# Two transfers per staged unit, and one reload per query tile, in a two-layer transformer kernel

## The chip, the cores and the metric

The kernel runs on one core of a Trainium2 chip. The core has TensorE (PE, matmuls), VectorE (DVE), ScalarE (ACT), GpSimd (POOL) and SyncE (SP), which only issues transfers, and 16 DMA engines that move data between HBM and the on-chip memory SBUF. Matmuls write to PSUM, eight banks of 128 x 512 floats. Transfers are issued from two queues here: SyncE's (q1 in the profile) and ScalarE's (q10). An engine works through its queue in order, so an instruction that waits, or a transfer being issued, holds what is behind it. The metric is the device time of one execution in microseconds.

## The reference

One sequence of 2048 tokens by 1024 features in float32 goes through two blocks. The part that the change touches is the first block's attention:

```
p = rmsnorm(x, norm1_g) @ w_in                 # 1024 -> u 256, dq dk dv 512 each, sq sk sv 256 each
a = pool_mixer(u)                              # trailing means, a small map per group
b = diff_attention(dq, dk, dv)                 # 4 heads: softmax(q1 k1^T) - lam * softmax(q2 k2^T), times v
c = stick_breaking_attention(sq, sk, sv)       # 4 heads of 64
x = x + concat(a, b, c) @ w_out
x = x + (silu(h2 @ w_gate) * (h2 @ w_up)) @ w_down      # h2 = rmsnorm(x, norm2_g)
x = rmsnorm(x, final_norm_g)
```

Both attentions are causal and scale by 1/8. The second block is a gated MLP over 128-token chunks and a retention branch, with a projection in and one out.

## The kernel before, in words

The sequence is cut in 4 chunks of 512 tokens. Matmuls keep float32 accuracy by splitting each operand in a rounded part (hi, written by ScalarE) and the rest (lo, VectorE's or GpSimd's subtraction) and adding three products: lines L1503, L1504 and L1505. Weights come as halves: `load_w` (L2620, L2627, SyncE) brings a raw half of 512 KB into one of three slots of RAW, `split_w` rounds it on ScalarE (L1749) and subtracts on GpSimd (L2529) into one of four or five places. `load_w` of half n waits for the split of half n-3. From about 1426 us on, halves that were kept in HBM are fetched again ready made (`fetch_w`, L2641, 1024 KB).

The projections of all four chunks come first (until about 580 us). A unit is one PSUM bank of 128 x 512 results. For a query or key unit (`store_qk`), ScalarE writes hi (L1823) and VectorE lo (L2135) into one of four slots of STG, hi in the first 512 columns of a slot, lo in the next; the 128 partitions hold two heads of 64 features each. Value units of the second attention are written the same way (`store_v`, L1831 and L2143); value units of the first attention stay whole. Then ScalarE's queue stores the slot to HBM scratch: `put_qk` (L1844 for queries, L1847 for keys) and `put_v` (L1861). One put is held back until the next unit is done (`put_later`).

- Queries: 4 transfers per unit, one for each of hi, lo and each head, into QS[6, 16, 64, hi/lo, head, 128].
- Keys: 4 transfers, into KS[6, 4, 128, head, 512], hi on the first 64 rows, lo on the last 64.
- Split values: 8 transfers, for hi/lo, head pair and 128-token tile.

There are 24 query units, 24 key units and 8 split value units. The attention goes over 96 tiles (4 chunks x 6 head pairs x 4 blocks of 128 queries). For each tile `load_q` (L2681, SyncE) brings the same 64 rows of 512 floats twice, onto partitions 0 to 63 and 64 to 127 of one of three slots of QQ, with two transfers. `load_k` (L2665) brings keys with hi on partitions 0 to 63 and lo on the others, and `scores` multiplies: QQ's hi part and then its lo part as the stationary side against hi and lo keys together (L1613, L1614). The softmax exponentials are on ScalarE (L1869), the turned probabilities are split by ScalarE (L1882) and VectorE (L2226).

The order of the work is one list, made when the program is built. The projections and everything after them run as one generator, `projections`, the attention as a second, `attention`. At each of 1484 places of the first, HALF_STEPS says how many half steps of the second are put there. Each engine takes its own instructions from this list in this order, and SyncE its transfers.

Of the kernel before, what the change touches and what calls it, by code (L numbers as in the profile page):

```python
# [9 lines left out]
F32 = mybir.dt.float32  # L10
# [3 lines left out]
ACT = mybir.ActivationFunctionType  # L14
ALU = mybir.AluOpType
# [4 lines left out]
CT = 512  # L20
NC = S // CT
# [50 lines left out]
class Signals:  # L72
# [6 lines left out]
    def inc(self, name, event, by=1):  # L79
        if name not in self.sems:  # L80
            self.sems[name] = self.ctx.enter_context(self.nc.semaphore(name))
        self.count[name] = self.count.get(name, 0) + by
        self.at[event] = (name, self.count[name])
        return self.sems[name], by

    def landed(self, name, event):
        return self.inc(name, event, 16)
# [127 lines left out]
def attention_cost(c):  # L215
# [2 lines left out]


HALF_STEPS = (  # L220
    "0000000000000000000000000000000000000000000000001200110120000010020200100101000000000100100100101210"
    "2122110001011003015000021100000020021110111002101121110100100021010011010111016100002001012010102002"
    "0001001000000001010000000000110222100210001001010000001110000220211002000100001010003002002010110101"
    "0010130131701131020000001011001000101001000001010000022021200210100010100000012000000201000010110001"
    "0031121021100110100001000001000100200001011020002130422112020001102020200000000000000000001000001010"
    "0001021000101010001010010011002010100000000010200000000111002001100100100100101111100000001100110000"
    "1002000200000000102001000010000000010102001003120111001221110011202022000011504100001010100000011000"
    "1011102000101001000000000011002000100011001120010000112020100101001000100001000102001002000212011102"
    "0021212001000100101010001011011000200100110012201210111200000100101000200110100300100002010022011010"
    "0010022100010010000100001000001001000011000010210100012000000001000002200000000000001111100000010000"  # L230
    "0000010000000101001000100020011001210002200201011000200000001200200000002001100200101200002100010200"
    "0101200021002000010020200211000100002111110002002200200110000000200210000001100010000101011211302400"
    "1000000001010011101000011000110100100311201031210000000001010001000100101000100000001001011101002000"
    "0010100000110101000010001002212100321110020000000000000000000000000010000000000100102010001201200111"
    "001100200120012100100010012001000001010120001010011102000101101110000000320100221004"
)


# [1070 lines left out]
def build(nc, I, const, out, scr):  # L1309
    with ExitStack() as ctx:  # L1310
        def sbt(name, n, dt=F32, stack=ctx):
            return stack.enter_context(nc.sbuf_tensor(name, [128, n], dt))

        BIG = sbt("BIG", 8192, FR)
        with ExitStack() as lay:
            STG = sbt("STG", 4096, FR, lay)
# [23 lines left out]
        PS = [ctx.enter_context(nc.psum_tensor(f"PS{i}", [128, 512], F32)) for i in range(8)]  # L1340
# [51 lines left out]
        QS, KS, VS, VW, US, YS, GP, GWS, WS, TB = [scr[n] for n in ("QS", "KS", "VS", "VW", "US", "YS", "GP", "GWS", "WS", "TB")]  # L1392
# [45 lines left out]
        def stage(s):  # L1438
            return STG[:, 1024 * s:1024 * s + 512], STG[:, 1024 * s + 512:1024 * s + 1024]

        def keys_of(kb):
            return KV[:, 2048 * kb:2048 * kb + 1024]

# [3 lines left out]
        def queries(s):  # L1447
            return QQ[:, 512 * s:512 * s + 512]
# [47 lines left out]
        inc, landed = sig.inc, sig.landed  # L1496


        def tensor_program(pe):
# [105 lines left out]
            def scores(c, x, r, j, qt, kb, w, ks, q, b, before):  # L1605
                for e in before:
                    on.wait_ge(*e)
                on.wait_ge("k", c, j, kb)
                on.wait_ge("q", c, j, qt)
                kk = keys_of(ks).rearrange("p (r t) -> p r t", r=2)  # L1610
                qq = queries(q).rearrange("p (a r t) -> p a r t", a=2, r=2)
                o = PS[4 + b][:, 0:w]
                pe.matmul(o, qq[:, 0, r, :], kk[:, r, 0:w], start=True, stop=False)  # L1613
                pe.matmul(o, qq[:, 1, r, :], kk[:, r, 0:w], start=False, stop=True).then_inc(*inc("scored", ("sc", x, r)))  # L1614
# [119 lines left out]
        def scalar_program(act):  # L1734
# [84 lines left out]
            def store_qk(c, u, kind, b, s, sbefore, ft):  # L1819
                on.wait_ge("mm", u)  # L1820
                for e in sbefore:
                    on.wait_ge(*e)
                act.activation(stage(s)[0], PS[b][:, :], ACT.Identity,  # L1823
                               scale=0.125 if kind == "q" else 1.0).then_inc(*inc("qkv_hi", ("qh", u)))

            def store_v(c, u, b, s, sbefore, ft, g):
                on.wait_ge("mm", u)
                for e in sbefore:
                    on.wait_ge(*e)
                to = stage(s)[0] if ft == 4 else stage(s)[0].bitcast(F32)  # L1830
                act.activation(to, PS[b][:, :], ACT.Copy).then_inc(*inc("qkv_hi", ("qh", u)))  # L1831

            def put_u(c, u, s, f):
                on.wait_ge("uc", u)
# [2 lines left out]
            def put_qk(c, u, kind, s, ft):  # L1837
                on.wait_ge("qh", u)
                on.wait_ge("ql", u)
                for a, src in enumerate(stage(s)):  # L1840
                    for r in range(2):
                        rows = src[64 * r:64 * r + 64, :].bitcast(F32)
                        if kind == "q":
                            act.dma_start(QS[ft, 4 * c:4 * c + 4, :, a, r, :].rearrange("q d t -> d q t"),  # L1844
                                          rows.rearrange("d (q t) -> d q t", q=4)).then_inc(*landed(f"s_st{s}", ("qst", u)))
                        else:
                            act.dma_start(KS[ft, c, 64 * a:64 * a + 64, r, :], rows).then_inc(*landed(f"s_st{s}", ("qst", u)))  # L1847

            def put_v(c, u, s, ft, g):
                on.wait_ge("qh", u)  # L1850
                if ft < 4:
                    act.dma_start(VW[:, c, :, g, :].rearrange("h p e -> p h e"),
                                  stage(s)[0].bitcast(F32).rearrange("p (h e) -> p h e", h=4)).then_inc(*landed(f"s_st{s}", ("qst", u)))
                    return
                on.wait_ge("ql", u)
                for a, src in enumerate(stage(s)):
                    for f in range(2):
                        view = src.rearrange("p (u n) -> p u n", u=2)[:, :, 128 * f:128 * f + 128]
                        by_head = VS[f, c, :, :, :, :].rearrange("p t a e -> p (t a e)").rearrange("p (t r a e) -> p t r a e", t=4, r=2, a=2)
                        for i in range(2):  # L1860
                            act.dma_start(by_head[:, 2 * g + i, :, a, :],  # L1861
                                          view[:, i, :].rearrange("p (r e) -> p r e", r=2).bitcast(F32)).then_inc(*landed(f"s_st{s}", ("qst", u)))

            def soft_exp(x, r, m, kb, w, b, s, before, m_after):
                nm, sm, _ = norm_cols(m, 4 * r + kb, 1)
# [141 lines left out]
        def vector_program(dve):  # L2007
# [122 lines left out]
                dve.tensor_copy(stage(s)[0].bitcast(F32), PS[b][:, :]).then_inc(*inc("u_out", ("uc", u)))  # L2130

            def store_qk(c, u, kind, b, s, sbefore, ft):
                hi, lo = stage(s)
                on.wait_ge("qh", u)
                dve.scalar_tensor_tensor(lo, PS[b][:, :], 0.125 if kind == "q" else 1.0, hi.bitcast(F32), ALU.mult,  # L2135
                                         ALU.subtract).then_inc(*inc("qkv_lo", ("ql", u)))

            def store_v(c, u, b, s, sbefore, ft, g):
                if ft < 4:
                    return  # L2140
                hi, lo = stage(s)
                on.wait_ge("qh", u)
                dve.tensor_tensor(lo, PS[b][:, :], hi.bitcast(F32), ALU.subtract).then_inc(*inc("qkv_lo", ("ql", u)))  # L2143

            def pool_load(c, u_stored, free):
                for e in free:
# [423 lines left out]
        def sync_program(sp):  # L2570
# [106 lines left out]
            def load_q(c, j, qt, s, after):  # L2677
                for e in after:
                    on.wait_ge(*e)
                for d in range(2):  # L2680
                    sp.dma_start(queries(s)[64 * d:64 * d + 64, :].bitcast(F32),  # L2681
                                 QS[j, 4 * c + qt, :, :, :, :].rearrange("d a r t -> d (a r t)")).then_inc(
                                     *landed(f"s_q{s}", ("q", c, j, qt)))

            def store_head(c, j):
                on.wait_ge("fm", c, j)
# [152 lines left out]
```

## Time and profile before

| | |
|---|---|
| median of 3 runs | 3711.91 us (3709.17 to 3713.26) |
| the profiled execution | 3712.05 us |
| its span, first to last instruction | 3710.3 us |
| mean granted TensorE clock | 0.988 |
| busy: PE, PEld, DVE, ACT, POOL | 97%, 83%, 51%, 45%, 22% of the span |
| SyncE's DMA queue q1 | 725.02 MB, 56.4% of 16 engines |
| ScalarE's DMA queue q10 | 35.67 MB, 3.5% of 16 engines |

PE is TensorE's matmuls, PEld its weight loads. Transfers being issued do not count as busy time of ScalarE or SyncE, though they keep its queue. A DMA share of 1 would be all 16 DMA engines with a packet in work all the time.

### The profile page before, as it was taken

What the parts mean: (1) busy time and instruction counts of PE and PEld (TensorE: products, weight loads), DVE (VectorE), ACT (ScalarE), POOL (GpSimd) and SP (SyncE); (2) the same over time, 40 slices, a digit from 0 to 9 for tenths busy, and PEclk for the clock granted to TensorE, in tenths of its full rate; (3) what the DMA queues carried; (4) which work ended last, traced back from release to release, by engine and by line L of the source; (5) the groups of instructions that cost most, each with busy time, mean ns of one, the idle gap of its engine ahead of it and who ended that gap; (6) DMA issues with size and microseconds to landing.
All of it is one profiled execution on the core that took longest, in us unless ns stands there. A gap on an engine that the chain in (4) does not pass through costs nothing.

```text
span 3710.3 us, 50941 instructions
## 1 busy us (share of the span) xinstructions
PE 3589.8 (97%) x19284; PEld 3081.8 (83%) x19284; DVE 1907.8 (51%) x4043; ACT 1664.5 (45%) x3393; POOL 807.5 (22%) x704
## 2 busy tenths in 40 slices
PE   7899999999999999999999999999999999999999
PEld 6788888777887898888888998888888988888788
DVE  4255654566657765445646555435477752111443
ACT  4344545545666454545544344435456532111322
POOL 3344443444454432000011011110000000000100
PEclk9999999999999999999999999999999999999999
DMA  6787677787776667545455456454454464555454
GB/s 191 215 251 214 187 216 275 258 283 268 267 255 227 239 230 288 188 165 196 167 183 177 165 204 216 160 203 170 165 213 136 150 240 184 190 183 205 171 189 153
DMA packets 328454, 763.95 MB, mean 206 GB/s; under 512 B 53265, under 2 KB 204817, under 8 KB 271890
## 3 DMA queue, kind: packets, MB, share of 16 engines
q1 hardware_dynamic: 267410, 725.02, 56.4%
q10 hardware_dynamic: 60800, 35.67, 3.5%
q8 instruction: 154, 2.52, 0.3%
q14 instruction: 90, 0.74, 0.1%
HBM read 586.25 MB, written 174.35 MB: 205 GB/s over the span
## 4 chain that ended last, share of the span: by engine, by line
PE 77%; DVE 5%; DMA 2%; ACT 2%; issue 1%; POOL 1%; SPq 0%; ACTq 0%; DVEq 0%
PE PS L1503 21%; PE PS L1505 21%; PE PS L1504 21%; PE PS L1622 3%; PE PS L1632 2%; PE PS L1613 2%; PE PS L1614 2%; PE PS L1646 2%; DMA XS<-in_w_ada 1%; PE PS L1581 1%; POOL WF L2529 1%; DVE XS L2309 0%; DVE BIG L2109 0%; ACTq L1861 0%; PE PS L1705 0%
## 5 line engine op out<-in xcount | busy, mean ns | idle before, releaser
L1503 PE MATMUL PS<-BIG,WF 128*128 128x512 f32 (+1 forms) x1792 | 688.4, 384 | 13.5 <-ACT BIG L1815 6.1
L1505 PE MATMUL PS<-BIG,WF 128*128 128x512 f32 (+1 forms) x1792 | 677.0, 378 | 0.0
L1504 PE MATMUL PS<-BIG,WF 128*128 128x512 f32 (+1 forms) x1792 | 676.6, 378 | 0.0
L2529 POOL TENSOR_TENSOR WF<-RAW,WF 128x512 fp32r<-128x512 f32 x380 | 509.3, 1365 | 620.0 <-ACT WF L1749 620.0
L1503 PE MATMUL PS<-WF,BIG 128*128 128x512 f32 (+1 forms) x1760 | 626.0, 356 | 8.2 <-DVE BIG L2098 4.6
L1505 PE MATMUL PS<-WF,BIG 128*128 128x512 f32 (+1 forms) x1760 | 611.3, 347 | 0.0
L1504 PE MATMUL PS<-WF,BIG 128*128 128x512 f32 (+1 forms) x1760 | 610.3, 347 | 0.0
L1503 PEld LDWEIGHTS PS<-BIG,WF 128*128 128x128 f32 x1792 | 343.0, 191 | 73.7 <-ACT BIG L1815 7.4
L1505 PEld LDWEIGHTS PS<-BIG,WF 128*128 128x128 f32 x1792 | 342.2, 191 | 62.9
L1504 PEld LDWEIGHTS PS<-BIG,WF 128*128 128x128 f32 x1792 | 343.2, 191 | 58.1
L1503 PEld LDWEIGHTS PS<-WF,BIG 128*128 128x128 f32 x1760 | 336.4, 191 | 52.3 <-ACT BIG L1799 5.2
L1505 PEld LDWEIGHTS PS<-WF,BIG 128*128 128x128 f32 x1760 | 336.1, 191 | 42.7
L1504 PEld LDWEIGHTS PS<-WF,BIG 128*128 128x128 f32 x1760 | 337.0, 191 | 40.4 <-issue 1.9
L1869 ACT ACTIVATE PP<-PS,SM 128x512 f32<-128x512 f32 (+3 forms) x320 | 199.1, 623 | 360.4 <-DVE SM L2194 349.7
L2556 POOL TENSOR_TENSOR AT<-XS,AT 128x512 fp32r<-128x512 f32 x88 | 115.9, 1317 | 1113.4 <-ACT AT L1932 1113.4
L1749 ACT ACTIVATE WF<-RAW 128x1024 fp32r<-128x1024 f32 x190 | 198.5, 1053 | 129.7 <-issue 90.4
L2194 DVE TENSOR_REDUCE SM<-PS 128x1 f32<-128x512 f32 (+3 forms) x320 | 193.2, 607 | 117.0 <-PE PS L1614 112.5
L2283 DVE TENSOR_TENSOR XH<-PS,XH 128x512 f32<-128x512 f32 x224 | 150.3, 686 | 199.9 <-PE PS L1505 199.8
L1932 ACT ACTIVATE AT<-XS 128x512 fp32r<-128x512 f32 x88 | 55.6, 632 | 397.9 <-DVE XS L2288 397.9
L1503 PE MATMUL PS<-WF,AT 128*128 128x512 f32 x584 | 233.5, 400 | 0.3 <-POOL WF L2529 0.3
L1505 PE MATMUL PS<-WF,AT 128*128 128x512 f32 x584 | 228.5, 391 | 0.0
L1504 PE MATMUL PS<-WF,AT 128*128 128x512 f32 x584 | 227.8, 390 | 0.0
(233 smaller groups left out, 6259.6 us busy)
## 6 DMA issues: line engine op xcount, KB each, us to landing
WF<-scratch_WS SPq DMA_DIRECT2D x264, 1024.0 KB, 5.0
scratch_WS<-WF SPq DMA_DIRECT2D x110, 1024.0 KB, 6.7
W<-scratch_WS SPq DMA_DIRECT2D x66, 1024.0 KB, 5.0
RAW<-in_w_in SPq DMA_DIRECT2D x84, 512.0 KB, 4.6
KV<-scratch_KS SPq DMA_DIRECT2D x60, 512.0 KB, 5.9
QQ<-scratch_QS SPq DMA_DIRECT2D x192, 128.0 KB, 5.1
XH<-in_x SPq DMA_DIRECT2D x32, 512.0 KB, 7.4
scratch_QS<-STG ACTq DMA_DIRECT2D x96, 128.0 KB, 4.0
```

Source lines behind the costliest of these rows:

```text
L1503: pe.matmul(o, Ah, Bh, start=first, stop=False)
L1504: pe.matmul(o, Ah, Bl, start=False, stop=False)
L1505: return pe.matmul(o, Al, Bh, start=False, stop=last)
L1613: pe.matmul(o, qq[:, 0, r, :], kk[:, r, 0:w], start=True, stop=False)
L1614: pe.matmul(o, qq[:, 1, r, :], kk[:, r, 0:w], start=False, stop=True).then_inc(*inc("scored", ("sc", x, r)))
L1622: m = pe.transpose(PS[6][:, 128 * i:128 * i + 128], src[:, 128 * i:128 * i + 128], ident)
L1749: act.activation(half_of(n)[0], rawp(n), ACT.Copy).then_inc(*inc("w_hi", ("w_hi", n)))
L1869: act.activation(probs(s)[:, 0:w], PS[4 + b][:, 0:w], ACT.Exp, bias=nm, accum_out=sm).then_inc(*inc("p_exp", ("ex", x, r)))
L2194: dve.tensor_reduce(nm, PS[4 + b][:, 0:w], AX, ALU.max, negate=True).then_inc(*inc("row_max", ("mx", x, r)))
L2283: dve.tensor_tensor(dst, PS[b][:, :], dst, ALU.add).then_inc(*inc("residual", ("res", u)))
L2529: pool.tensor_tensor(lo, rawp(n)[:, 512 * i:512 * i + 512], hi.bitcast(F32), ALU.subtract).then_inc(*inc("w_lo", ("w_lo", n, i)))
L2556: pool.tensor_tensor(lo, gated(s), hi.bitcast(F32), ALU.subtract).then_inc(*inc("act_lo", ("al", u)))
```

## The change

1. Queries: ScalarE and VectorE write the staged unit as four query blocks of 128 with hi and lo side by side in each, so that one transfer per head stores both: 2 per unit. The scratch becomes QS[6, 16, 64, head, 256], and `scores` reads QQ as (head, hi/lo, token) in place of (hi/lo, head, token).
2. Keys: staged as before; one transfer per head stores hi and lo: 2 per unit. The lo part is a plain subtraction now.
3. Split values: staged as eight blocks of 64 with hi and lo side by side; one transfer per head pair: 2 per unit.
4. `load_q` is one transfer. Its source is the 64 rows with a leading dimension of 2 and a step of 0, its destination all 128 partitions.
5. HALF_STEPS has other digits at 366 of its 1484 places; their sum is 742 in both.

```diff
+        def stage_parts(s):
+            return STG[:, 1024 * s:1024 * s + 1024]
+
+        def stage_q(s):
+            q4 = stage_parts(s).rearrange("p (q a t) -> p q a t", q=4, a=2)
+            return q4[:, :, 0, :], q4[:, :, 1, :]
+
+        def stage_v(s):
+            m8 = stage_parts(s).rearrange("p (m a e) -> p m a e", m=8, a=2)
+            return m8[:, :, 0, :], m8[:, :, 1, :]
...
-                qq = queries(q).rearrange("p (a r t) -> p a r t", a=2, r=2)
+                qq = queries(q).rearrange("p (r a t) -> p a r t", a=2, r=2)
...
-                for a, src in enumerate(stage(s)):
-                    for r in range(2):
-                        rows = src[64 * r:64 * r + 64, :].bitcast(F32)
-                        if kind == "q":
-                            act.dma_start(QS[ft, 4 * c:4 * c + 4, :, a, r, :].rearrange("q d t -> d q t"),
-                                          rows.rearrange("d (q t) -> d q t", q=4)).then_inc(*landed(f"s_st{s}", ("qst", u)))
-                        else:
-                            act.dma_start(KS[ft, c, 64 * a:64 * a + 64, r, :], rows).then_inc(*landed(f"s_st{s}", ("qst", u)))
+                for r in range(2):
+                    rows = stage_parts(s)[64 * r:64 * r + 64, :].bitcast(F32)
+                    if kind == "q":
+                        act.dma_start(QS[ft, 4 * c:4 * c + 4, :, r, :].rearrange("q d x -> d q x"),
+                                      rows.rearrange("d (q x) -> d q x", q=4)).then_inc(*landed(f"s_st{s}", ("qst", u)))
+                    else:
+                        act.dma_start(KS[ft, c, :, r, :].rearrange("(a d) t -> d a t", a=2),
+                                      rows.rearrange("d (a t) -> d a t", a=2)).then_inc(*landed(f"s_st{s}", ("qst", u)))
...
-                for a, src in enumerate(stage(s)):
-                    for f in range(2):
-                        view = src.rearrange("p (u n) -> p u n", u=2)[:, :, 128 * f:128 * f + 128]
-                        by_head = VS[f, c, :, :, :, :].rearrange("p t a e -> p (t a e)").rearrange("p (t r a e) -> p t r a e", t=4, r=2, a=2)
-                        for i in range(2):
-                            act.dma_start(by_head[:, 2 * g + i, :, a, :],
-                                          view[:, i, :].rearrange("p (r e) -> p r e", r=2).bitcast(F32)).then_inc(*landed(f"s_st{s}", ("qst", u)))
+                view = stage_parts(s).rearrange("p (i f x) -> p i f x", i=2, f=2).bitcast(F32)
+                for f in range(2):
+                    act.dma_start(VS[f, c, :, 2 * g:2 * g + 2, :, :].rearrange("p i a e -> p i (a e)"),
+                                  view[:, :, f, :]).then_inc(*landed(f"s_st{s}", ("qst", u)))
...
-                dve.scalar_tensor_tensor(lo, PS[b][:, :], 0.125 if kind == "q" else 1.0, hi.bitcast(F32), ALU.mult,
-                                         ALU.subtract).then_inc(*inc("qkv_lo", ("ql", u)))
+                if kind == "q":
+                    hi, lo = stage_q(s)
+                    dve.scalar_tensor_tensor(lo, PS[b][:, :].rearrange("p (q t) -> p q t", q=4), 0.125, hi.bitcast(F32), ALU.mult,
+                                             ALU.subtract).then_inc(*inc("qkv_lo", ("ql", u)))
+                else:
+                    hi, lo = stage(s)
+                    dve.tensor_tensor(lo, PS[b][:, :], hi.bitcast(F32), ALU.subtract).then_inc(*inc("qkv_lo", ("ql", u)))
...
-                for d in range(2):
-                    sp.dma_start(queries(s)[64 * d:64 * d + 64, :].bitcast(F32),
-                                 QS[j, 4 * c + qt, :, :, :, :].rearrange("d a r t -> d (a r t)")).then_inc(
-                                     *landed(f"s_q{s}", ("q", c, j, qt)))
+                src = QS[j, 4 * c + qt, :, :, :].rearrange("(b d) r x -> b d (r x)", b=1).broadcast_to([2, 64, 512])
+                sp.dma_start(queries(s).bitcast(F32), src).then_inc(*landed(f"s_q{s}", ("q", c, j, qt)))
```

## Rows read from the trace of the kernel before

**Rows 1.** Windows, by stage: window, its us, busy (count) by engine, clock, DMA share, GB/s.
```profile
150.00:465.00 315.00, 289.21 (x1585) 253.46 (x1586) 179.10 (x409) 147.22 (x347) 131.06 (x108) 0.96 0.72 216
465.00:1010.00 545.00, 514.23 (x2604) 433.01 (x2603) 316.67 (x615) 285.61 (x595) 244.23 (x198) 0.97 0.76 260
1010.00:1400.00 390.00, 377.61 (x2217) 329.89 (x2217) 257.20 (x569) 222.61 (x452) 172.24 (x149) 1.00 0.68 235
1400.00:2830.00 1430.00, 1419.52 (x7581) 1215.54 (x7580) 768.45 (x1552) 683.75 (x1443) 155.26 (x164) 1.00 0.54 189
...
sum 3710.00, PE 3589.82 PEld 3081.83 DVE 1907.77 ACT 1664.48 POOL 807.52; mean PE 598.30 PEld 513.64 DVE 317.96 ACT 277.41 POOL 134.59
```
**Rows 2.** Waits of TensorE, 60 to 600 us: in total, times, longest.
```profile
PE PS L1613 <- ACT PP L1869: 7.4, 2, 3.8
...
PE PS L1646 <- DVE PT L2226: 6.2, 2, 4.8
PE PS L1503 <- ACT BIG L1815: 6.1, 1, 6.1
PE PS L1613 <- DMA QQ<-scratch_QS: 4.9, 1, 4.9
```
**Rows 3.** Windows, the four chunk ends of the projections: the first and the sum.
```profile
140.00:180.00 40.00, 28.26 (x190) 27.00 (x190) 18.01 (x32) 11.00 (x22) 11.02 (x8) 0.83 0.73 221
...
sum 160.00, PE 132.85 PEld 123.79 DVE 90.48 ACT 68.84 POOL 58.72; mean PE 33.21 PEld 30.95 DVE 22.62 ACT 17.21 POOL 14.68
```
**Rows 4.** Timeline of ScalarE at two chunk ends: start, us, what, [idle before].
```profile
148.49 15.96 ACTq L1861 DMA_DIRECT2D scratch_VS<-STG  x16
164.50 1.06 ACT L1749 ACTIVATE WF<-RAW 128x1024 fp32r<-128x1024 f32 x1 [15.47 <-issue]
...
436.16 5.26 ACTq L1861 DMA_DIRECT2D scratch_VS<-STG  x8
441.52 0.60 ACT L1882 ACTIVATE PT<-PS 128x512 fp32r<-128x512 f32 x1 [5.11 <-issue]
```
**Rows 5.** Issues of the four transfers: ns min/median/max, first and last start.
```profile
L1844 ACTq DMA_DIRECT2D scratch_QS<-STG x96: 582/640/1230, 41.9 to 550.0; - x96
L1847 ACTq DMA_DIRECT2D scratch_KS<-STG x96: 452/620/1629, 74.8 to 562.0; - x96
L1861 ACTq DMA_DIRECT2D scratch_VS<-STG x64: 364/492/2397, 148.5 to 578.8; - x64
...
L2681 SPq DMA_DIRECT2D QQ<-scratch_QS x192: 444/597/2223, 150.3 to 2804.4; - x192
```
**Rows 6.** The staging writes, same columns.
```profile
L1823 ACT ACTIVATE STG<-PS x48: 577/597/601, 36.9 to 554.0; 128x512 fp32r<-128x512 f32 x48
L2135 DVE SCALAR_TENSOR_TENSOR STG<-PS,STG x48: 674/691/693, 37.5 to 554.6; 128x512 fp32r<-128x512 f32 x48
```
**Rows 7.** Issue to landing of query loads (L2681), then of weight fetches (L2641).
```profile
DMA to landing us min/median/max: 2.4/5.1/13.9
...
DMA to landing us min/median/max: 4.6/5.0/13.6
```
**Rows 8.** DMA in 1794 to 1799 us: packets, MB, share of 16 engines.
```profile
q1 hardware_dynamic: 160, 0.26, 19.3%
```
**Rows 9.** DMA, 150 to 465 us, two rows, then 465 to 1010 us, one.
```profile
q1 hardware_dynamic: 36125, 48.31, 49.3%
...
QQ<-scratch_QS SPq DMA_DIRECT2D x49, 128.0 KB, 5.1
...
QQ<-scratch_QS SPq DMA_DIRECT2D x48, 128.0 KB, 6.5
```
**Rows 10.** Weight splits and raw loads: the splits, SyncE's wait, landing of L2627.
```profile
L1749 ACT ACTIVATE WF<-RAW x190: 1040/1056/1069, 10.9 to 1422.0; 128x1024 fp32r<-128x1024 f32 x190
...
SPq L2627 <- POOL WF L2529: 673.7, 139, 20.8
...
DMA to landing us min/median/max: 2.1/4.4/12.2
```

More of the change, by code:

```diff
@@ L220 @@
 HALF_STEPS = (
[L221 to L225, printed above, removed]
@@ L226 @@
-    "0001021000101010001010010011002010100000000010200000000111002001100100100100101111100000001100110000"
-    "1002000200000000102001000010000000010102001003120111001221110011202022000011504100001010100000011000"
+    "0000000000000000000000000000000000000000000000001011110010001020020000200010100000001020000102100110"
+    "2121100010001202114020301101020000100120111011001121010002000101110101101101111000300210010200100102"
+    "0002000000010200110001010000010122101110001100000000201101100211221001000010000001000002040012100100"
@@ L228 @@
+    "1000231200201740220011000100000000010100100010111001031021210101010002000010010001000010100010001002"
+    "1210020210000200101100000100010100000110001002002021320222200002022012010000100010000000000001000011"
+    "0000102010010010111000000000021001202000000010200001000011000200100000020010001000320000110000110000"
+    "1100200100000010101000001000010000010102001003111111001221110011202022000011504100001010100000011000"
     "1011102000101001000000000011002000100011001120010000112020100101001000100001000102001002000212011102"
-    "0021212001000100101010001011011000200100110012201210111200000100101000200110100300100002010022011010"
@@ L230 @@
-    "0010022100010010000100001000001001000011000010210100012000000001000002200000000000001111100000010000"
-    "0000010000000101001000100020011001210002200201011000200000001200200000002001100200101200002100010200"
+    "0021212001000100101010001011011000200100110012201210101010101100011101011050000100001000211121012011"
+    "0010000100000100000100010001110000000011010001020010002100000001100000200000000000001111101000000000"
+    "0000010000000101001000100020011001100202220101100000200000001200200000002001100200101200002100010200"
@@ L232 @@
     "0101200021002000010020200211000100002111110002002200200110000000200210000001100010000101011211302400"
     "1000000001010011101000011000110100100311201031210000000001010001000100101000100000001001011101002000"
-    "0010100000110101000010001002212100321110020000000000000000000000000010000000000100102010001201200111"
-    "001100200120012100100010012001000001010120001010011102000101101110000000320100221004"
+    "0010100000110010100100200002012202301110000100100000000000000000000100000000000200101102010010200111"
@@ L236 @@
+    "001100200120012100100010012001000000001010101010100200300001011220001001110001112015"
 )
@@ L1822, in store_qk @@
                     on.wait_ge(*e)
-                act.activation(stage(s)[0], PS[b][:, :], ACT.Identity,
-                               scale=0.125 if kind == "q" else 1.0).then_inc(*inc("qkv_hi", ("qh", u)))
+                if kind == "q":
+                    act.activation(stage_q(s)[0], PS[b][:, :].rearrange("p (q t) -> p q t", q=4), ACT.Identity,
+                                   scale=0.125).then_inc(*inc("qkv_hi", ("qh", u)))
+                else:
+                    act.activation(stage(s)[0], PS[b][:, :], ACT.Identity).then_inc(*inc("qkv_hi", ("qh", u)))
             def store_v(c, u, b, s, sbefore, ft, g):
@@ L1829, in store_v @@
                     on.wait_ge(*e)
-                to = stage(s)[0] if ft == 4 else stage(s)[0].bitcast(F32)
-                act.activation(to, PS[b][:, :], ACT.Copy).then_inc(*inc("qkv_hi", ("qh", u)))
+                if ft == 4:
+                    act.activation(stage_v(s)[0], PS[b][:, :].rearrange("p (m e) -> p m e", m=8), ACT.Copy).then_inc(
+                        *inc("qkv_hi", ("qh", u)))
+                else:
+                    act.activation(stage(s)[0].bitcast(F32), PS[b][:, :], ACT.Copy).then_inc(*inc("qkv_hi", ("qh", u)))
             def put_u(c, u, s, f):
@@ L1839, in put_qk @@
                 on.wait_ge("ql", u)
-                for a, src in enumerate(stage(s)):
-                    for r in range(2):
-                        rows = src[64 * r:64 * r + 64, :].bitcast(F32)
-                        if kind == "q":
-                            act.dma_start(QS[ft, 4 * c:4 * c + 4, :, a, r, :].rearrange("q d t -> d q t"),
-                                          rows.rearrange("d (q t) -> d q t", q=4)).then_inc(*landed(f"s_st{s}", ("qst", u)))
-                        else:
-                            act.dma_start(KS[ft, c, 64 * a:64 * a + 64, r, :], rows).then_inc(*landed(f"s_st{s}", ("qst", u)))
+                for r in range(2):
[3 more added lines that the diff above has]
+                                      rows.rearrange("d (q x) -> d q x", q=4)).then_inc(*landed(f"s_st{s}", ("qst", u)))
+                    else:
+                        act.dma_start(KS[ft, c, :, r, :].rearrange("(a d) t -> d a t", a=2),
+                                      rows.rearrange("d (a t) -> d a t", a=2)).then_inc(*landed(f"s_st{s}", ("qst", u)))
             def put_v(c, u, s, ft, g):
@@ L2132, in store_qk @@
             def store_qk(c, u, kind, b, s, sbefore, ft):
-                hi, lo = stage(s)
                 on.wait_ge("qh", u)
-                dve.scalar_tensor_tensor(lo, PS[b][:, :], 0.125 if kind == "q" else 1.0, hi.bitcast(F32), ALU.mult,
-                                         ALU.subtract).then_inc(*inc("qkv_lo", ("ql", u)))
+                if kind == "q":
+                    hi, lo = stage_q(s)
+                    dve.scalar_tensor_tensor(lo, PS[b][:, :].rearrange("p (q t) -> p q t", q=4), 0.125, hi.bitcast(F32), ALU.mult,
+                                             ALU.subtract).then_inc(*inc("qkv_lo", ("ql", u)))
+                else:
+                    hi, lo = stage(s)
+                    dve.tensor_tensor(lo, PS[b][:, :], hi.bitcast(F32), ALU.subtract).then_inc(*inc("qkv_lo", ("ql", u)))
             def store_v(c, u, b, s, sbefore, ft, g):
@@ L2140, in store_v @@
                     return
-                hi, lo = stage(s)
+                hi, lo = stage_v(s)
                 on.wait_ge("qh", u)
-                dve.tensor_tensor(lo, PS[b][:, :], hi.bitcast(F32), ALU.subtract).then_inc(*inc("qkv_lo", ("ql", u)))
+                dve.tensor_tensor(lo, PS[b][:, :].rearrange("p (m e) -> p m e", m=8), hi.bitcast(F32),
+                                  ALU.subtract).then_inc(*inc("qkv_lo", ("ql", u)))
             def pool_load(c, u_stored, free):
@@ L2832 @@
     scr = {}
-    for name, shape in (("QS", [6, 16, 64, 2, 2, 128]), ("KS", [6, NC, 128, 2, CT]), ("VS", [2, NC, 128, 4, 2, 128]), ("VW", [4, NC, 128, 4, 128]),
+    for name, shape in (("QS", [6, 16, 64, 2, 256]), ("KS", [6, NC, 128, 2, CT]), ("VS", [2, NC, 128, 4, 2, 128]), ("VW", [4, NC, 128, 4, 128]),
                         ("US", [2, 128, S + 16]), ("YS", [S, D]), ("GP", [1, D]), ("GWS", [128, 4, 128]), ("WS", [SPLIT - KEPT, 128, 2048]), ("TB", [2, 128, 1024])):
```

## The prediction

> **What bounds the kernel now.** I read the stages first [rows 1], the five of them by busy time, granted clock and DMA share, to see where TensorE leaves time at all. It is busy for 3589.82 of 3710 us, so about 120 us are idle, and they are not spread evenly: from 1400 to 2830 us only 10 us of 1430 are idle, while 150 to 465 us has 25.8 idle of 315 and 465 to 1010 us has 30.8 of 545. Those two stages also have the highest DMA share (0.72 and 0.76, against 0.54 later). The change touches what runs there: the projections store queries, keys and values until about 579 us [rows 5], and the query loads run from 150 to 2804 us.
>
> Next, what TensorE waits for in 60 to 600 us [rows 2]. Four rows matter: 7.4 us for ScalarE's exponentials, 6.2 us for a VectorE piece that itself waited for ScalarE, 6.1 us for ScalarE's rounding of the next activations, and 4.9 us for the first query load. The four 40 us windows at the ends of the projection chunks hold 27.2 us of TensorE idle (160 minus 132.85), 11.7 of them at the first end, where the granted clock is 0.83 [rows 3]. The ScalarE timeline says why [rows 4]: at 148.49 us its queue issues 16 value stores in a row and this takes 15.96 us, with the weight split behind it starting after 15.47 us of idle; at 436.16 us eight of them take 5.26 us and hold the next turned-probability eviction for 5.11 us. So ScalarE's queue, filled by store issues, is what ends waits at the chunk ends. Elsewhere the tensor engine bounds.
>
> **The stores, part by part.** Removed: per query unit 4 issues become 2 (96 to 48), per key unit the same (96 to 48), per split-value unit 8 become 2 (64 to 16). By the medians 48 x 0.640 + 48 x 0.620 + 48 x 0.492 = 84 us of ScalarE queue time before 580 us [rows 5]. For queries and keys no long TensorE wait stands behind the issues, and I give them 0 (0 to 5 us gain). For values, three of four issues go at each chunk end. The waits of TensorE that trace to a late ScalarE there are 7.4 + 6.2 + 6.1 = 19.7 us [rows 2]; three quarters is 15 us gained. Bounds: 5 us, if the pieces queued behind are late for the next reason (VectorE's own lo parts and softmax maxima are next), and 20 us. What is stored has the same bytes. Rows of a value store grow from 256 to 512 bytes and those of a query store from 512 to 1024, which only shortens the queue-10 traffic; 0 to 3 us of DMA engine time, not counted.
>
> The staging writes now go to 4 or 8 blocks in place of one run (query and value units), and the key's subtraction drops a multiply by 1. The nearest rows are the writes themselves, 0.597 us on ScalarE and 0.691 us on VectorE [rows 6]. No row shows the blocked form; at 10% each way over 56 units it is 3 us on either engine, hidden under TensorE's gemms at all but the chunk ends. I take 0, plus or minus 1.
>
> **The query reload.** Two issues of 128 KB become one of 256 KB, 192 to 96, 0.6 us of SyncE each [rows 5]; SyncE mostly waits for a free buffer, so this is worth 0 (at best half a microsecond on the first load). But the shape of the source changes. Before, each transfer counts 64 rows outermost. In a quiet stretch [rows 8] two such loads left 160 packets: 128 rows of 2 KB, and 32 more, 16 for each load, so each one ran on all sixteen DMA engines. The new source counts 2 outermost, with a step of 0, then 64 rows; only below it lie the equal parts that sixteen engines would need. No row of before shows such a transfer. The two ends are: still sixteen engines, then nothing is lost; or one half per engine, then two engines carry 128 KB each where each engine carried 16 KB per tile before. I take the second, because in the rows each of these loads is split by its outermost count.
>
> What that second end costs. Two engines get 112 KB more per tile. Price from three rows. Slope between landings: a 1024 KB fetch has 64 KB per engine and lands at best in 4.6 us, a 128 KB query load has 8 KB and lands at best in 2.4 us [rows 7], so 56 KB take 2.2 us and 112 KB take 4.4 us. The SyncE queue's own rate in this stage: 48.31 MB in 49.3% of 16 x 315 us is 19.4 GB/s per engine, so 5.9 us [rows 9]. The quiet stretch: 0.26 MB in 19.3% of 16 x 5 us is 17 GB/s, 6.8 us [rows 8].
>
> Stage 150 to 465 us: an engine is in use for 0.72 x 315 = 227 us [rows 1]. 49 issues are 24.5 tiles [rows 9]. The two engines then need 227 + 24.5 x 4.4 = 335 us up to 227 + 24.5 x 5.9 = 372 us, which is 20 to 57 us more than there are; I take the middle, 38. Every transfer of the queue, weights and keys too, lands only when those two engines have done their share, so their backlog delays all. What TensorE has in hand against it is the lead of the weight loads: there are three raw slots, so a load goes out when the split three before it is done (SyncE waits 673.7 us for that), 190 splits in 1411 us is 7.4 us each, two of them are 15 us, less 4.4 us of landing: 10 us of lead [rows 10]. So 38 - 10 = 28 us lost. Bounds: 0 if the other packets get quicker once fourteen engines are idler, and 79 us at 6.8 us without any lead.
>
> First tile: TensorE already waits 4.9 us for it [rows 2]; it lands about 5 us later, +5 (0 to 7).
>
> Stage 465 to 1010 us: 0.76 x 545 = 414 us, plus 24 tiles at 4.4 to 5.9 is 520 to 556 us of 545 [rows 1, 9]. Full but not clearly over, with the lead already spent: +8 (0 to 32). Stage 1010 to 1400: about 13 tiles, 0.68 x 390 + 13 x 5.9 = 342 of 390, fits. After that 0.54 and the queries of one tile are needed far later than loaded: 0.
>
> ScalarE waits in order for a raw weight, so when one is late its exponentials are late too; that multiplies stalls and is why I don't go to the low end.
>
> The Trainium skill speaks against the new reload, in "DMA: Bandwidth & Descriptors", the table of rules for kernel authors and the section on why a DMA increments its semaphore by 16: the engines used are the largest number up to 16 that divides the slowest dimension of both sides, and a leading zero-stride broadcast of c copies keeps the whole transfer on at most c engines. That is 2 here. The count of 16 small packets per load agrees with it for 64 rows; that a count of 2 gives two engines no row of before can show.
>
> **The places.** 366 of 1484 digits of the order string differ, the sum is 742 in both, and at no slot is the attention more than 8 half steps behind or 5 ahead of its old position. It moves pieces against each other at the scale of single waits. All of TensorE's idle time is 120 us, and a part of it is what such a move can shift; I take 0, between -6 and +8.
>
> **Sum.** 28 + 5 + 8 - 15 = +26 us. The profiled execution took 3712.05 us (span 3710.3, 1.75 around it), which is 0.1 above the median 3711.91. So 3738 us.
>
> **Rivals.** Below 0.2% (7.4 us) no difference from no change can be told.
> (A) Forecast, the two engines back up: 3738. Its own range is 3720 to 3790. For it: DMA shares of 0.72 and 0.76 before anything is added. Against: a share counts waiting inside packets too, and that may give way.
> (B) The other side: the reload still runs over sixteen engines, and shorter ScalarE queues at the chunk ends decide. Place: ScalarE's queue at the four chunk ends, where the value stores of 148.49 and 436.16 us are two. Price: 15 us, a microsecond from SyncE. 3712 - 16 = 3696. It decides as soon as the query load adds no more than 15 us in all. For it: [rows 4]. Against: the leading count.
> (C) Two engines, but their backlog is mostly absorbed: price 4.4 us, 20 - 10 = +10 in the first stage, +5 first tile, 0 later, -15: 3712. For it: query loads themselves have slack, TensorE waited for one only once in 96 tiles [rows 2]. Against: the loads queued behind them are what is late.
> Every top end at once would be 3712 + 79 + 5 + 32 - 5 = 3823, not in the range.
>
> **Chances.** A 0.66, B 0.18, C 0.16. From A 0.64 slower and 0.02 same, from B 0.16 faster and 0.02 same, from C 0.05 faster, 0.06 same, 0.05 slower: faster 0.21, same 0.10, slower 0.69. Range 3698 to 3788: it leaves out the low half of B and the top of A.
>
> **What would show it.** Packets: if two engines carry a load, it leaves 2 small packets and not 16 beside its 128 rows, so some 2900 fewer in the trace from the loads alone, and the median landing of a query load goes from 5.1 us to 10 or more in the first stages. TensorE's first-query wait grows from 4.9 to about 10 us. In 150 to 465 us the mean DMA share falls while SyncE's and ScalarE's waits for raw weights grow; idle of TensorE in this stage goes from 26 to over 45 us. The value stores at the chunk ends show 4 issues in under 4 us. The forecast is wrong if query loads land in 5 to 6 us (B), or if they land late and the raw weights still come before ScalarE asks for them (C).

## The result, and the profile after

| | before | after |
|---|---|---|
| median | 3711.91 us | 3725.81 us (3722.69 to 3730.83, 5 runs) |
| ratio to before | | 1.0041, 95% interval 1.003 to 1.0052 |
| profiled execution, span | 3710.3 us | 3720.9 us |
| TensorE busy, idle | 3589.8, 120.5 us | 3586.8, 134.1 us |
| mean granted clock | 0.988 | 0.989 |

The change made the kernel 0.41% slower. That small number is what is left of gains and losses that are larger than it, as the experiments show. Windows over the stages of after, columns as in [rows 1]:

```profile
150.00:465.00 315.00, 278.01 (x1533) 239.03 (x1532) 171.04 (x398) 141.44 (x327) 125.38 (x105) 0.97 0.68 213
465.00:1010.00 545.00, 511.62 (x2606) 431.14 (x2605) 316.70 (x618) 287.84 (x609) 242.52 (x198) 0.98 0.74 258
1010.00:1400.00 390.00, 380.51 (x2225) 332.35 (x2224) 257.42 (x572) 224.66 (x453) 177.93 (x153) 0.99 0.69 239
1400.00:2830.00 1430.00, 1415.32 (x7540) 1210.07 (x7539) 762.31 (x1539) 678.22 (x1433) 152.91 (x164) 1.00 0.55 190
...
```

Idle of TensorE in the first stage went from 25.8 to 37.0 us, while the mean DMA share fell from 0.72 to 0.68 and the rate from 216 to 213 GB/s: less is moved per microsecond, and TensorE waits. The four chunk ends went the other way, from 27.2 to 9.9 us idle (160 minus 150.12, against [rows 3]):

```profile
140.00:180.00 40.00, 32.46 (x214) 30.21 (x214) 17.73 (x32) 12.76 (x27) 11.59 (x10) 0.91 0.63 202
...
sum 160.00, PE 150.12 PEld 137.11 DVE 97.29 ACT 79.92 POOL 61.25; mean PE 37.53 PEld 34.28 DVE 24.32 ACT 19.98 POOL 15.31
```

The timeline of ScalarE shows the reason for that, where [rows 4] had 15.96 us of issues and 15.47 of idle:

```profile
147.27 3.03 ACTq L1875 DMA_DIRECT2D scratch_VS<-STG  x4
150.35 1.06 ACT L1760 ACTIVATE WF<-RAW 128x1024 fp32r<-128x1024 f32 x1 [2.54 <-issue]
```

What TensorE waits for between 60 and 600 us has changed its names (compare [rows 2]; in after, L1643 is the product of probabilities and values, L1624 the scores, L1514 the first of the three products of the projections):

```profile
PE PS L1643 <- ACT PTW L1902: 14.2, 3, 10.2
PE PS L1624 <- DMA QQ<-scratch_QS: 10.0, 2, 7.5
PE PS L1514 <- POOL WF L2548: 6.5, 5, 2.8
```

ScalarE waits for raw weights in after as below; before it waited 7.9 us (3 times) and 8.3 us (2 times) for the same two transfers:

```profile
ACT WF L1760 <- DMA RAW<-in_w_in: 69.6, 13, 12.8
...
ACT WF L1760 <- DMA RAW<-in_w_out: 12.9, 4, 5.0
```

TensorE's wait of 10.2 us stands behind the longest of these. Here are SyncE, ScalarE and TensorE in order. SyncE starts to issue raw loads at 252.94 us; the first of them lands at 266.8, ScalarE has idled 12.83 us by then, and the probabilities queued behind its weight split (L1902) are late for TensorE:

```profile
252.94 17.93 SPq L2646 DMA_DIRECT2D RAW<-in_w_in  x4
...
266.83 1.06 ACT L1760 ACTIVATE WF<-RAW 128x1024 fp32r<-128x1024 f32 x1 [12.83 <-DMA RAW<-in_w_in]
...
268.20 0.76 PE L1643 MATMUL PS<-KVF,PTW 128*128 128x128 f32 x2 [10.23 <-ACT PTW L1902]
```

The longest issue of a raw load in this stage is 8.04 us, at 348.47 us, the second of the two in this row of SyncE:

```profile
345.05 11.46 SPq L2646 DMA_DIRECT2D RAW<-in_w_in  x2
```

Does one reload run on two engines? The same quiet stretch as [rows 8], around a single query load of after (1802.5 to 1808.8 us; the first row is the GB/s of 40 slices):

```profile
GB/s 0 0 0 0 0 0 0 0 0 0 26 0 0 26 26 26 52 52 52 52 52 52 52 52 52 52 26 52 52 52 52 52 52 52 52 52 52 52 52 52
...
q1 hardware_dynamic: 102, 0.21, 8.6%
```

The rate stands at 52 GB/s in most slices, and after nearly 5 us only 102 of the load's 128 packets are out. 0.21 MB in 8.6% of 16 x 6.3 us is 24 GB/s per engine in use, so 52 GB/s is two engines. The packets themselves, in the trace, start two at a time and 0.08 us apart, from 1804.08 to 1809.83 us; so from its issue at 1802.78 us this load took 7 us, where the median from issue to landing of the two loads in [rows 8] was 2.7. The count of small packets (4 bytes, of which each load of [rows 8] left sixteen) agrees exactly: in the traces they fell from 34578 to 29394, by 5184. The 144 store issues that are gone make 144 x 16 = 2304; the other 2880 are 192 x 16 minus 96 x 2. Two per load remain, not sixteen. The profile also no longer gives a landing time for the 96 loads ("256.0 KB" with nothing behind it).

The Trainium skill's rule ("DMA: Bandwidth & Descriptors", the rules for kernel authors: a leading zero-stride broadcast of c copies stays on at most c engines) is borne out here: c is 2, and two engines carry it.

### The profile page after: what moved, and what is told of

It reads as the page before. It is cut to its first block, busy times and chain, and to the rows that moved or that the text cites. A ratio compares the mean times of both kernels' runs of the same rounds, so it can differ in the third digit from the quotient of the medians.

```text
span 3720.9 us, 50701 instructions
## 1 busy us (share of the span) xinstructions
PE 3586.8 (96%) x19284; PEld 3074.3 (83%) x19284; DVE 1903.1 (51%) x4043; ACT 1666.0 (45%) x3393; POOL 804.0 (22%) x704
## 4 chain that ended last, share of the span: by engine, by line
PE 78%; DMA 8%; DVE 6%; ACT 3%; issue 2%; POOL 2%; SPq 1%; ACTq 0%; DVEq 0%
PE PS L1514 21%; PE PS L1516 21%; PE PS L1515 21%; PE PS L1633 3%; PE PS L1643 2%; DMA XS<-in_w_ada 2%; PE PS L1625 2%; DMA RAW<-in_w_in 2%; PE PS L1624 2%; PE PS L1657 2%; POOL WF L2548 1%; PE PS L1592 1%; DMA QQ<-scratch_QS 1%; DMA RAW<-in_w_out 1%; DMA GROW<-in_gmlp_ln_g 1%
## 5 line engine op out<-in xcount | busy, mean ns | idle before, releaser
L1514 PE MATMUL PS<-BIG,WF 128*128 128x512 f32 (+1 forms) x1792 | 684.3, 382 | 12.0 <-POOL WF L2548 5.4
L1514 PE MATMUL PS<-WF,BIG 128*128 128x512 f32 (+1 forms) x1760 | 626.2, 356 | 10.3 <-DVE BIG L2112 4.6
L1514 PEld LDWEIGHTS PS<-BIG,WF 128*128 128x128 f32 x1792 | 339.4, 189 | 73.3 <-issue 6.1
L1516 PEld LDWEIGHTS PS<-BIG,WF 128*128 128x128 f32 x1792 | 338.8, 189 | 62.6
L1515 PEld LDWEIGHTS PS<-BIG,WF 128*128 128x128 f32 x1792 | 339.7, 190 | 57.8
L1514 PEld LDWEIGHTS PS<-WF,BIG 128*128 128x128 f32 x1760 | 336.2, 191 | 55.0 <-ACT BIG L1810 6.7
L1514 PE MATMUL PS<-WF,AT 128*128 128x512 f32 x584 | 233.5, 400 | 2.4 <-DVE XH L2302 1.8
## 6 DMA issues: line engine op xcount, KB each, us to landing
QQ<-scratch_QS SPq DMA_DIRECT2D x96, 256.0 KB
scratch_QS<-STG ACTq DMA_DIRECT2D x48, 256.0 KB, 5.2
```

The costliest lines, as they stand in the source:

```text
L1514: pe.matmul(o, Ah, Bh, start=first, stop=False)
L1515: pe.matmul(o, Ah, Bl, start=False, stop=False)
L1516: return pe.matmul(o, Al, Bh, start=False, stop=last)
```

## The experiments

All ratios are to the kernel before, run beside each experiment on the same chip, where its median was 3709.6 to 3711.1 us; each experiment has 4 to 11 executions. Diffs are against after or before, as named.

**Two reload transfers again, all else as after.**

```diff
-                src = QS[j, 4 * c + qt, :, :, :].rearrange("(b d) r x -> b d (r x)", b=1).broadcast_to([2, 64, 512])
-                sp.dma_start(queries(s).bitcast(F32), src).then_inc(*landed(f"s_q{s}", ("q", c, j, qt)))
+                for d in range(2):
+                    sp.dma_start(queries(s)[64 * d:64 * d + 64, :].bitcast(F32),
+                                 QS[j, 4 * c + qt, :, :, :].rearrange("d r x -> d (r x)")).then_inc(
+                                     *landed(f"s_q{s}", ("q", c, j, qt)))
```

> The changed kernel, with the query reload again as two transfers of 64 rows; stores, staging and places stay as changed. Theory 1 (one reload runs on two of the sixteen DMA engines, and these back up): the median query landing is back at 5 us, waits for raw weights shrink, and the time falls by 25 to 35 us from 3725.8, to about 3695 (0.996 of before, the store part's 15 us gained). Rival 2 (the reload is absorbed, the new places lose what is lost): stays within 5 us of 3725.8. Rival 3 (the merged stores themselves are slow): the same.

Measured: 3664.41 us, 0.9879 (0.9863 to 0.9895). The reload costs 61 us, about twice what was expected for this run. Its windows:

```profile
150.00:465.00 315.00, 311.39 (x1720) 271.31 (x1719) 206.34 (x448) 162.62 (x373) 146.29 (x119) 0.99 0.75 236
465.00:1010.00 545.00, 521.49 (x2656) 439.32 (x2655) 310.60 (x606) 301.29 (x612) 248.58 (x202) 0.98 0.77 269
1010.00:1400.00 390.00, 380.03 (x2227) 332.22 (x2226) 252.59 (x580) 213.56 (x456) 165.19 (x144) 0.99 0.71 246
1400.00:2830.00 1430.00, 1421.60 (x7622) 1219.02 (x7621) 787.49 (x1601) 694.32 (x1446) 144.02 (x154) 1.00 0.52 183
```

In the first stage 3.6 us are idle where after has 37.0, and the DMA share is 0.75: the engines do more per microsecond once all sixteen are used. Over the span, idle is 85.5 us (3662.2 minus 3576.7) against 134.1. So 48.6 us of the difference between the two spans, 58.7, is idle time; the other 10 is TensorE's busy time for the same 19284 matmuls (3576.7 against 3586.8), with a mean granted clock of 0.991 against 0.989; what made the busy time longer was not tried.

**One reload transfer alone, on the kernel before.** The mirror image of the diff above, with the scratch layout of before.

> The kernel before, with only the query reload as one transfer whose source counts 2 outermost with a step of 0; stores and places of before. Theory 1: 25 to 45 us slower, 3737 to 3757 (1.007 to 1.012), since the places of before were not laid for it; 2880 small packets fewer. Rivals 2 and 3: within 5 us of 3711.9.

Measured: 3774.14 us, 1.0167 (1.0152 to 1.0183), 63 us slower. The small packets are 2880 fewer (31698). The reload alone does it. That the new places or the merged stores were what lost the time (the expectations' rivals 2 and 3) is ruled out.

**The order string of before, on after.**

> The changed kernel with the order string of before. Theory 1, where the places are worth nothing on their own: within 6 us of 3725.8. Rival 2 (the new places lose 10 us or more): 3700 to 3716. Rival 4 (the new places repair a part of what the reload costs): 3732 to 3745.

Measured: 3753.14 us, 1.0113 (1.0098 to 1.0128). This is above every range that was named. The new places gain 27 us here; the forecast's 0 falls, and so does the rival that had them as the loss.

**One reload transfer whose source counts 64 outermost.** Two lines on after; the keys' rows go to 2d and 2d+1 so that they meet the same queries.

```diff
-                src = QS[j, 4 * c + qt, :, :, :].rearrange("(b d) r x -> b d (r x)", b=1).broadcast_to([2, 64, 512])
+                src = QS[j, 4 * c + qt, :, :, :].rearrange("(d b) r x -> d b (r x)", b=1).broadcast_to([64, 2, 512])
...
-                        act.dma_start(KS[ft, c, :, r, :].rearrange("(a d) t -> d a t", a=2),
+                        act.dma_start(KS[ft, c, :, r, :].rearrange("(d a) t -> d a t", a=2),
```

> The changed kernel, but the reload's one transfer puts the two copies of a row on neighbouring partitions (2d and 2d+1), so its source counts 64 outermost and the step of 0 stands inside; the keys' rows are stored in the same order. Theory 1 (what matters is the outermost count): sixteen engines again, 18 small packets less than two transfers would leave and no query backlog: time as with two transfers or 1 to 3 us better, about 3693. If the repeated read itself were slow and not the outermost count: as the changed kernel, 3726.

Measured: 3658.14 us, 0.9857 (0.9842 to 0.9872), the lowest median of all runs here and faster than both kernels; from the 3664.41 us with two transfers (0.9863 to 0.9895) it is not told apart. The same bytes are read twice with the same step of 0, in one transfer; only the order of the two dimensions, and with it that of the keys' rows, differs from after. The loads land again, and each leaves sixteen small packets: 30738, which is 1536 = 96 x 16 fewer than with two transfers (the 18 in the expectation was a slip). Issue and landing of its 96 query loads:

```profile
L2700 SPq DMA_DIRECT2D QQ<-scratch_QS x96: 519/525/2254, 147.0 to 2759.1; - x96
...
DMA to landing us min/median/max: 2.8/5.7/14.4
```

What two busy engines do to the queue behind them shows in the raw loads of 150 to 465 us, issue and landing. After:

```profile
L2646 SPq DMA_DIRECT2D RAW<-in_w_in x42: 363/404/8039, 167.7 to 459.0; - x42
...
DMA to landing us min/median/max: 3.5/8.7/19.1
```

and with the source counting 64 outermost:

```profile
L2646 SPq DMA_DIRECT2D RAW<-in_w_in x49: 367/368/777, 153.6 to 463.7; - x49
...
DMA to landing us min/median/max: 3.5/4.7/11.8
```

The same holds for every transfer that SyncE issues. Counted in all the traces here, from 150 to 465 us: in the three kernels whose reloads all count 2 outermost, 19 to 24 issues last over 2 us each and all issues together take 128 to 152 us. In the other eleven it is 0 or 1 such issue and 62 to 81 us. One of these eleven is the run below with two transfers in the first chunk alone: 1 in this stage, then 8 between 465 and 1010 us, where its other reloads begin.

**The merged stores alone** (after with two reload transfers and the order string of before).

> The merged stores and their staging alone: two reload transfers as before, order string of before. What is known: changed kernel with two reloads 3664 (0.988), with old places 3753 against 3726. If the places' worth is the same 27 us with or without the backlog (theory 1b), this comes to 3664 + 27 = 3691 (0.995), and the stores alone are worth 20 us. If the places only repair what the one reload broke (rival 4), it comes to 3664 to 3670. If the merged stores are worth only the 5 us of the low bound, 3706.

Measured: 3685.05 us, 0.9925 (0.9913 to 0.9938), a gain of 25 us, and the places add 17 (by the ratios) to 21 (by the medians) to it (3664.41).

**The new places alone, on before.**

> The kernel before with the new order string alone. Theory 1b (places worth 27 us whatever the rest): about 3685 (0.993). Rival 4 (they fit only the changed transfers): 3705 to 3725.

Measured: 3707.20 us, 0.9992 (0.9984 to 1.0001), not told from no change. So what the places gain elsewhere, some 20 to 27 us by the medians, depends on the rest of the change.

**The value part alone, on before.** Staging in eight blocks, `put_v` with two transfers:

```diff
-                for a, src in enumerate(stage(s)):
-                    for f in range(2):
...
+                view = stage_parts(s).rearrange("p (i f x) -> p i f x", i=2, f=2).bitcast(F32)
+                for f in range(2):
+                    act.dma_start(VS[f, c, :, 2 * g:2 * g + 2, :, :].rearrange("p i a e -> p i (a e)"),
+                                  view[:, :, f, :]).then_inc(*landed(f"s_st{s}", ("qst", u)))
```

> The kernel before with the value part alone: staging in eight blocks, two transfers per unit instead of eight. The prediction's step gives all of the stores' gain to this: 10 to 20 us, 3692 to 3702. If the gain is the query and key stores' instead: 3706 to 3712.

Measured: 3694.60 us, 0.9957 (0.9943 to 0.9971), 15 us on a before of 3709.64. TensorE is idle at the chunk ends for 12.7 us in its profile, not 27.2. Of its three waits in [rows 2] that the forecast put down to ScalarE's queue, 7.4, 6.2 and 6.1 us, there are 2.8, 4.4 and none left between 60 and 600 us.

```profile
sum 160.00, PE 147.28 PEld 133.07 DVE 94.45 ACT 77.77 POOL 66.41; mean PE 36.82 PEld 33.27 DVE 23.61 ACT 19.44 POOL 16.60
```

**Two reload transfers in the first chunk only**, on after: `load_q` takes the two transfers of the first diff if c is 0, the one otherwise.

> The changed kernel, with the two-transfer reload for the 24 tiles of the first chunk only; the other 72 tiles keep the one transfer. Theory 1 by stages (28 + 5 of 41 us fall in the first chunk): most of the 61 us comes back, 3675 to 3690. If the weight-fed stage from 465 us on pays as much: 3695 to 3710.

Measured: 3682.88 us, 0.9926 (0.9914 to 0.9939). Of the 61 us, 43 belong to the 24 tiles of the first chunk and 18 to the other 72. From 1400 us on this run is idle for 10.5 us of 1430, like before:

```profile
1400.00:2830.00 1430.00, 1419.51 (x7609) 1215.90 (x7608) 781.80 (x1587) 689.82 (x1449) 144.12 (x154) 1.00 0.54 186
```

**The query and key stores alone, on before.**

> The kernel before with the query and key stores merged alone (and the query staging in four blocks); value stores, reload and places of before. The stores together measured 3685 (0.9925) and the values alone 3694.6 (0.9957). If the two parts add up, this comes to 3700 to 3703 (0.997 to 0.998). If both shorten the same waits at the chunk ends, it comes to 3695 to 3699. The prediction's 0 to 5 us: 3706 to 3711.

Measured: 3705.20 us, 0.9988 (0.9979 to 0.9997): 4 to 6 us, less than the expected additive 8 to 11. With the values' 15 this makes 19 to 21 where both together measured 25; the intervals, some 5 us to each side for the two larger, don't tell these apart.

**The same with the new places, and the value part with the new places.**

> The same with the new order string. The new places are worth 2.4 us on the kernel before and 21 us on top of both merged stores. If their worth needs the value stores short: 3698 to 3702, no more than 3 us below the run before. If it needs the query and key stores short: 3680 to 3685.

> The kernel before with the value part and the new order string. If the places' worth needs the value stores short: 3674 to 3680, 15 to 20 us below 3694.6. If it needs the query and key stores short: 3690 to 3695.

Measured: 3701.60 us, 0.9978 (0.9969 to 0.9987), and 3674.12 us, 0.9902 (0.9889 to 0.9916). The new places gain 3.6 us on the first, which the intervals don't tell from nothing, and 20.5 us on the second: they need short value stores. Up to 465 us TensorE is busy for 433.63 us with the new places and 425.93 without, both with the value part; between 465 and 1010 us for 520.28 and 515.16. Which pieces moved where to bring this was not followed.

**The reload whose source counts 64 outermost, with the old places.**

> The changed kernel with the reload on neighbouring partitions (source counting 64 outermost) and the order string of before. Only the outermost count differs from the changed kernel with old places (3753), so theory 1: 68 us less, about 3680 to 3685, and 20 to 25 us above the same with the new places (3658).

Measured: 3678.68 us, 0.9921 (0.9907 to 0.9934). From 3753.14 that is 74 us, the cost of the outermost count with these places, and the new places gain 20.5 more.

The parts together, as differences of medians in us against the kernel before. The intervals are 3 to 6 us to each side:

```
                                 old places        new places
stores and reload as before         0                 -3
query and key stores               -6                 -9
value stores                      -15                -37
all stores                        -25                -47
all stores, reload 64 outermost   -32                -53
all stores, reload 2 outermost    +42                +14
reload 2 outermost alone          +63           not tried
```

## Why the prediction was right, and where its terms were not

The sign, the mechanism and the range held: 3726 lies inside 3698 to 3788 and in the forecast case's own 3720 to 3790. The sum, +26 against +14 measured, is close by luck: the reload cost 20 us more than its terms, and the query and key stores and the places brought some 10 and 21 us that the sum had as 0. In numbers, 61 - 15 - 10 - 21 is +15, where the forecast had 41 - 15.

1. **Two DMA engines carry the reload: right.** It stood on the outermost count, which no row of before could show. 52 GB/s in a quiet stretch, two small packets per load, and the run with the dimensions swapped show it.
2. **The price per tile: right.** 4.4 to 5.9 us for 112 KB more; the 24 GB/s of the quiet stretch of after make it 4.8 us, the 0.08 us per row of 2 KB 4.5.
3. **What it costs the stages: too small.** 28 + 5 in the first chunk and 8 later, 41 us in all; measured 43 and 18, 61 in all (63, 68 and 74 by the other three pairs). The term that was too small is the loss in the stages, and the step behind it that fits least is the subtraction of 10 us of lead. That lead is an average: in before a raw load was already late for ScalarE five times, so the backlog meets moments without a lead. Without the subtraction the first chunk would have been 38 + 5 = 43 us, which is what was measured; but no run varied the lead, so this is argued and not shown, and it leaves the 18 against 8 us later open. The runs show two things that the sum had no term for. The issue of a transfer itself takes longer: 8.04 us for a raw load in the first stage, where the longest with two reload transfers was 0.59, and 152 us for all of SyncE's issues in this stage against 78.5. A transfer that isn't issued gives the other fourteen engines no work. And 10 of the 59 us between the two spans are busy time of TensorE, not idle time. Whether the repaired stores left less room for the backlog can't be told: 63 us without them and 68 with them, at the same places, lie within their intervals.
4. **The value stores: right,** 15 us expected from three quarters of 19.7, 15 measured alone (11 to 21 by the interval). The waits of TensorE that traced back to ScalarE's queue gave the size, and they are what shrank.
5. **The query and key stores: 0 (up to 5) expected, 4 to 6 alone** and up to 10 beside the values. The staging in blocks cost nothing, as expected: the medians of the writes are 0.598 and 0.692 us in after, 0.597 and 0.691 in [rows 6].
6. **The places: 0 expected (-6 to +8), about -20 to -27 measured with the short value stores** and -2.4, not told from 0, without them. The bounds were taken from a digit count and from the idle time of before, and missed that places can be laid for something else in the same change. This error is as large as that of the reload and of the other sign, and hid it.
7. **First tile:** the wait for it went from 4.9 us to 7.5, 2.6 more where 5 were expected; a second wait for a query load, later in the stage, makes it 10.0 in total. One of the forecast's own signs did not come: idle in the first stage did not pass 45 us as written, it reached 37.0; the stores' gain falls in the same windows. Nor could the landing of the query loads be read as the forecast wanted, since the profile gives none.

Rival B was half right as well: the shorter ScalarE queues that it rests on are worth 25 us with old places and 47 with new ones, and they decide once the reload runs on sixteen engines. Only the leading count kept them from deciding.

## What to carry to other kernels

Where one transfer reads its source twice by a step of 0, put that dimension inside and the rows, here 64, outside; the order of these two dimensions was worth 68 us of 3726 (1.0041 against 0.9857). Price a slow transfer by what is queued behind it, not by its own slack: TensorE waited for a query load only twice, 10 us in all, and lost 61. Before a gain or loss is put down to one part of a change, take out each part alone: 15, 10, 21 and -61 us were under a difference of 14 us.

## What the runs showed of the hardware that was not expected

- SyncE's issue of a transfer takes longer when the transfers before it are far behind: a raw load took up to 8.04 us to issue in 150 to 465 us of after, against 0.59 before and with two reload transfers, and 0.78 with the source counting 64 outermost. It isn't peculiar to transfers on two engines: near 49 us, before any query load, a pair of raw loads takes 8.90 us to issue in the kernel before as well. How much must be behind for it was not tried.

```profile
48.71 8.90 SPq L2627 DMA_DIRECT2D RAW<-in_w_in  x2
```

- ScalarE's issues were slow too where many came in a row: 16 value stores took 15.96 us [rows 4], a microsecond each against a median of 0.492 [rows 5]; four take 3.03, 0.76 each. Why they are slower there was not tried.
- The transfers here that use two of the sixteen engines leave two packets of 4 bytes and no landing time in the profile, where the same loads otherwise leave sixteen and have one; that is a quick way to look for such transfers in a trace.
- Two engines moved rows of 2 KB at 26 GB/s each, one row in 0.08 us, steadily, with no other transfer in work.
